# Attention blocks of two heads in turn, with the values of both heads made in one call, in a two-layer hybrid encoder trunk

## The reference, cut to what matters

```
def one_block(args):
    qi, bi = args
    qchunk = (bi * ATTN_BLOCK + jnp.arange(ATTN_BLOCK)) // CHUNK
    s = jnp.einsum('bqhd,bkhd->bhqk', qi, k, preferred_element_type=jnp.float32)
    s = jnp.where(kchunk[None, :] <= qchunk[:, None], s, -jnp.inf)
    p = jax.nn.softmax(s, axis=-1).astype(v.dtype)
    return jnp.einsum('bhqk,bkhd->bqhd', p, v)
```

## Time and profile before

| | |
|---|---|
| median of 3 runs | 1456.1 us (1455.23 to 1457.14) |
| the profiled execution's own time | 1454.87 us |
| its span in the trace | 1453.0 us |
| PE busy | 1366.1 us, 94% of the span |
| DVE, ACT, POOL busy | 774.2, 510.5, 541.4 us |
| mean granted PE clock | 0.958 of full |

### The profile page before, as it was taken

One profiled execution on the slowest core, in us unless ns is written; L12 is line 12 of the kernel. 1 busy time (PEld: TensorE's weight loads), 2 busy tenths in 40 slices (PEclk: granted clock), 3 DMA queues, 4 the chain that ended last, 5 costly groups with the idle time before them and its releaser, 6 DMA issues. The chain is left out here.

```text
span 1453.0 us, 17110 instructions
## 1 busy us (share of the span) xinstructions
PE 1366.1 (94%) x6812; PEld 1019.3 (70%) x6812; DVE 774.2 (53%) x1370; ACT 510.5 (35%) x778; POOL 541.4 (37%) x328
## 2 busy tenths in 40 slices
PE   5989899998999999899899999999899999989986
PEld 2546676776888888688655576767688888868865
DVE  5885767645667666532368646574533333321125
ACT  2523134435433333322233422253443333332322
POOL 0630100565544444344446110055744444434432
PEclk9999999898999999899999999999999999999988
DMA  9345733021665555454314451002133232322321
GB/s 384 137 116 164 155 107 117 16 87 41 212 191 180 187 192 191 139 195 153 119 60 117 78 72 45 30 30 73 44 102 101 87 102 88 101 72 88 97 63 58
DMA packets 64798, 166.76 MB, mean 115 GB/s; under 512 B 14288, under 2 KB 26960, under 8 KB 64208
## 3 DMA queue, kind: packets, MB, share of 16 engines
q1 hardware_dynamic: 64720, 165.68, 36.8%
HBM read 160.04 MB, written 5.62 MB: 114 GB/s over the span
## 5 line engine op out<-in xcount | busy, mean ns | idle before, releaser
L2044 POOL TENSOR_TENSOR ring_r<-ring,scr_r 128x1024 fp32r<-128x1024 f32 x148 | 360.2, 2435 | 441.0 <-ACT scr_r L1913 273.6
L442 PE MATMUL bank<-ym_r,scr_r 128*128 128x512 f32 x704 | 280.7, 399 | 5.3 <-DVE hm_r L1565 4.7
L444 PE MATMUL bank<-hm_r,scr_r 128*128 128x512 f32 x704 | 280.0, 398 | 0.0
L443 PE MATMUL bank<-ym_r,ring_r 128*128 128x512 f32 x704 | 277.2, 394 | 0.0
L442 PE MATMUL bank<-scr_r 128*128 128x512 f32 x480 | 197.5, 411 | 25.3 <-issue 14.2
L443 PE MATMUL bank<-scr_r,ring_r 128*128 128x512 f32 x480 | 191.0, 398 | 0.0
L1581 DVE SCALAR_TENSOR_TENSOR scr<-bank,pb,scr 128x511 f32<-128x511 f32 x88 | 66.0, 750 | 212.7 <-ACT scr L1906 212.6
L512 PE MATMUL bank<-hm,ring 128*128 128x512 f32 x352 | 168.3, 620 | 0.0
L1067 DVE SCALAR_TENSOR_TENSOR ada<-ada,silu_c 128x1024 f32<-128x1024 f32 x80 | 135.0, 1690 | 50.1 <-DMA ada<-in_w_ada 50.1
L442 PEld LDWEIGHTS bank<-ym_r,scr_r 128*128 128x128 f32 x704 | 132.7, 189 | 38.2 <-issue 6.3
L444 PEld LDWEIGHTS bank<-hm_r,scr_r 128*128 128x128 f32 x704 | 132.6, 188 | 33.2
(11 more groups left out here) (324 smaller groups left out, 1795.8 us busy)
## 6 DMA issues: line engine op xcount, KB each, us to landing
ring<-in_w_up SPq DMA_DIRECT2D x88, 512.0 KB, 3.6
ada<-in_w_ada SPq DMA_DIRECT2D x80, 512.0 KB, 3.6
ring<-in_w_down SPq DMA_DIRECT2D x44, 512.0 KB, 3.5
ring<-in_w_in SPq DMA_DIRECT2D x34, 512.0 KB, 4.5
scr<-in_w_ada SPq DMA_DIRECT2D x16, 512.0 KB, 14.3
ring<-in_w_out SPq DMA_DIRECT2D x16, 512.0 KB, 3.6
pa<-in_par_a SPq DMA_DIRECT2D x2, 2144.5 KB, 12.9
xa<-in_x SPq DMA_DIRECT2D x1, 2048.0 KB, 8.1
```

Source lines behind the costliest of these rows:

```text
L442: first = mm(dst, w_hi, x_hi, start=start, stop=False)
L443: mm(dst, w_lo, x_hi, start=False, stop=False)
L444: return first, mm(dst, w_hi, x_lo, start=False, stop=stop)
L2044: G.tensor_tensor(ring_r[:, at, :], ring[:, at, :], high[:, at, :].bitcast(F32), ALU.subtract)\
```

## The change

The blocks are taken in another order: the two heads of a pair in turn, query block by query block. `block_of(i)` gives heads 0 and 1 for i = 0 to 7, and heads 2 and 3 for i = 8 to 15, so b runs 0,0,1,1,2,2,3,3 twice where it ran 0,1,2,3 four times. The values of two blocks are made in one call `values(j)`, with the matmuls of the two heads in turn, each into its half of bank 5, and evicted by one instruction of 128 rows. A second place for a turned block is the memory of `iota`; what S5 needs of `iota` is copied out once on POOL in layer 0.

```diff
+def block_of(i):
+    return 2 * (i // 8) + i % 2, (i % 8) // 2
...
+        turned = [ptt, c_f("iota")]
...
                 def scores(i):
-                    h, b = i // NB, i % NB
+                    h, b = block_of(i)
...
-                def values(i):
-                    h, b = i // NB, i % NB
-                    pe.wait_ge(S["pt_out"], l * 16 + i + 1)
-                    if i >= 1:
-                        pe.wait_ge(S["pv_out"], l * 16 + i)
+                def values(j):
+                    h, b = block_of(2 * j)
+                    pe.wait_ge(S["pt_out"], l * 16 + 2 * j + 2)
+                    if j >= 1:
+                        pe.wait_ge(S["pv_out"], l * 8 + j)
                     for k in range(b + 1):
-                        last = mm(banks[5][64 * (h % 2):64 * (h % 2) + 64, b * P:(b + 1) * P],
-                                  vb[:, k, h * HD:(h + 1) * HD], ptt[:, k * P:(k + 1) * P],
-                                  start=(k == 0), stop=(k == b))
+                        for hp in range(2):
+                            last = mm(banks[5][64 * hp:64 * hp + 64, b * P:(b + 1) * P],
+                                      vb[:, k, (h + hp) * HD:(h + hp + 1) * HD], turned[hp][:, k * P:(k + 1) * P],
+                                      start=(k == 0), stop=(k == b))
                     last.then_inc(S["pv_mm"], 1)
...
-                    if i >= 3:
-                        values(i - 3)
+                    if i >= 4 and i % 2 == 0:
+                        values(i // 2 - 2)
...
-                    if i >= 3:
-                        h, b = (i - 3) // NB, (i - 3) % NB
-                        rows = slice(64 * (h % 2), 64 * (h % 2) + 64)
-                        a.wait_ge(S["pv_mm"], l * 16 + i - 2)
-                        A(ym[rows, 2 + h // 2, b * P:(b + 1) * P], banks[5][rows, b * P:(b + 1) * P], ACT.Identity)\
+                    if i >= 4 and i % 2 == 0:
+                        j = i // 2 - 2
+                        h, b = block_of(2 * j)
+                        a.wait_ge(S["pv_mm"], l * 8 + j + 1)
+                        A(ym[:, 2 + h // 2, b * P:(b + 1) * P], banks[5][:, b * P:(b + 1) * P], ACT.Identity)\
                             .then_inc(S["pv_out"], 1)
                     if 2 <= i < 18:
-                        b = (i - 2) % NB
+                        b = block_of(i - 2)[1]
                         a.wait_ge(S["pt_mm"], l * 16 + i - 1)
-                        A(ptt[:, 0:(b + 1) * P], banks[4][:, 0:(b + 1) * P], ACT.Identity).then_inc(S["pt_out"], 1)
+                        if i >= 4:
+                            a.wait_ge(S["pv_mm"], l * 8 + i // 2 - 1)
+                        A(turned[i % 2][:, 0:(b + 1) * P], banks[4][:, 0:(b + 1) * P], ACT.Identity).then_inc(S["pt_out"], 1)
...
-                steps = c_f("iota").rearrange("p (o c s) -> p o c s", o=1, s=SC)[:, :, :, 0]
+                steps = steps_t[:, :].rearrange("p (o c) -> p o c", o=1)
+                if l == 0:
+                    ch.link(G.tensor_copy(steps, c_f("iota").rearrange("p (o c s) -> p o c s", o=1, s=SC)[:, :, :, 0]))
```

More of the change, by code:

```diff
@@ L166, in trunk @@
         neg_half = sb("neg_half", [P, 16])
+        steps_t = sb("steps_t", [P, NSC])
         scr, scr_r = twins("scr", [P, SCRATCH])
@@ L668, in turn @@
                 def turn(i):
-                    b = i % NB
+                    b = block_of(i)[1]
                     pe.wait_ge(S["sc_norm"], l * 16 + i + 1)
@@ L798, in glu @@
                     pe.wait_ge(S["s5_gelu"], l * CT + CT)
-                    pe.wait_ge(S["pv_out"], l * 16 + 16)
+                    pe.wait_ge(S["pv_out"], l * 8 + 8)
                     wg = p_a("w_glu").rearrange("p (k n) -> p k n", n=GW)
@@ L1262, in attend @@
                 def attend(i):
-                    b, q = i % NB, i % 2
+                    b, q = block_of(i)[1], i % 2
                     if i < 16:
@@ L1271, in attend @@
                     if i:
-                        b, q = (i - 1) % NB, (i - 1) % 2
+                        b, q = block_of(i - 1)[1], (i - 1) % 2
                         v.wait_ge(S["sc_exp"], l * 16 + i)
@@ L1855, in _ @@
                 evict(AT[AU1])
-                a.wait_ge(S["pv_out"], l * 16 + 16)
+                a.wait_ge(S["pv_out"], l * 8 + 8)
                 for k in (2, 3):
```

## The result

| | before | after |
|---|---|---|
| median of the runs on one chip | 1455.76 us (8 runs) | 1445.69 us (8 runs) |
| ratio | | 0.9922 (0.9904 to 0.9941) |
| the profiled execution's own time, span | 1454.87, 1453.0 us | 1448.5, 1446.6 us |

The changed kernel is faster: the ratio is 11.4 us of 1455.76 (8.6 to 14.0). The forecast was 8.8 us less, so the direction was right and the size too small. By the ratio the time is 1444.4 us, just under the low end of the range, 1444.5. The first interval still holds 8.8 us, the second doesn't.

What follows compares the result with a forecast made beforehand. PE was taken to set the pace during attention. Layer 0 saves 0.26 + 3.48 = 3.74 us and layer 1 1.56 + 3.48 = 5.04, together 8.8, giving 1447.3 us from a median of 1456.1; range 1444.5 to 1452.0.

Steps and rivals of the forecast that it cites:

- Scores and transposes stay the same in number: PE's attention work: scores and transposes unchanged in number, transposes priced at 0.15 + 0.11 us each; only their order changes.
- 2.04 us earlier: PE up to `project(AT[I0], 0)`: fewer scores, transposes and values calls ahead of it, so it comes 2.04 us earlier.
- Values, 5.52 us a layer less: Values calls on PE: a two-head call costs what a one-head call cost, 5.52 us a layer for 11.04.
- The halves don't overlap: Rival on the values calls: only 8 x 0.14 us a layer saved, 1454.9 us in all; chance 0.04.
- each alternation pays the start of a call: Rival on the values calls: 0.36 us for each of 40 matmuls, 3.4 us a layer more, 1462.8 us; chance 0.04.
- The wait in `attend(7)`: PE's wait for ACT passes to L674; chain 0.48 us longer; ends 0.26 us earlier in layer 0, 1.56 in layer 1.
- After the wait, 3.48 us each: PE from the end of the `attend(7)` wait: the remaining 3.48 us of each layer's saving is kept there.
- The clock behind the longer wait in layer 1: Rival: PE's clock falls after the `attend(7)` wait, 1.7 to 3.4 us come back, 1449.0 to 1450.7 us; chance 0.13.
- DVE did not take over: Rival at `level(1)`, layer 0: HGRN2 levels follow DVE, layer keeps 1.2 of 3.74 us, 1449.8 us; chance 0.09.
- The full move: Rival on the `attend(7)` wait: `s_k` lands earlier by PE's gain, both layers get 5.52 us, 1445.1 us; chance 0.05.

Runs made afterwards that it cites:

- the loops changed round: Changed kernel with the two loops of `values(j)` swapped, all matmuls of one head before the other's: 1448.17 us, 0.9938 of the kernel before.
- the order alone: Kernel before with only the new order of blocks, values still one head a call: 1458.64 us, ratio 1.0019.

## Why the prediction was right or wrong

**The mechanism was right, its size too small, and two terms of the sum failed.** "Scores and transposes stay the same in number" priced the transposes as unchanged; they got 0.9 us a layer cheaper. And "2.04 us earlier" counted no clock ahead of the wait; in layer 1 the clock gave 1.6 us.

**Values, 5.52 us a layer less: right.** A call for two heads costs 0.37, 0.59, 0.81, 1.03 us, on the price taken from L834 to 0.01 us. "The halves don't overlap" and "each alternation pays the start of a call" are out; the loops changed round show the overlap once more.

**Transposes: first failed step.** The prediction priced a call at 0.15 + 0.11 each, and this 0.15 is in the chain only where a values call stands ahead. Half of the values calls are gone, so in every odd `attend(i)` with scores the transposes now stand right behind the scores, at 0.11, 0.22, 0.33 and 0.44 us for one to four. The first such row was there before the change, in `attend(2)` of layer 1, from the timeline of PE:

```profile
822.41 0.27 PE L674 MATMUL bank<-cf,scr 128*128 128x128 f32 x1
822.52 2.74 PE L512 MATMUL bank<-hm,ring 128*128 128x512 f32 x6
```

The next matmul starts 0.11 us behind the transpose. `attend(3)` and `attend(5)` save 0.15 each ahead of `project(AT[I0], 0)`, `attend(9)`, `attend(11)`, `attend(13)` and `attend(15)` behind the wait: 0.30 and 0.60 us a layer. By the sum it is thus 2.34 us up to I0 and 4.08 behind the wait, for 2.04 and 3.48. With the clock alike, the traces show 2.32 in layer 0 and 4.05 behind the wait in layer 1.

**"2.04 us earlier" up to `project(AT[I0], 0)`: second failed step.** In layer 1 it was 3.97. Of that 2.33 are work; the other 1.64 are clock, since the three matmuls behind the kernels went from 4.35 to 2.84 us and the last kernel matmuls from 0.53 to 0.40. The trace of before had them at the lower clock, in full view of the timeline, and I priced the clock only as a cost that could come on top, never as one that could go.

**The wait in `attend(7)`: right in place and releaser; its chain right, its start not.** It passed to the transposes and its releasing chain grew: from POOL's start to its end it took 48.07 - 41.88 = 6.19 us before and 46.89 - 40.16 = 6.73 after in layer 0, 45.29 - 39.11 = 6.18 and 41.91 - 35.15 = 6.76 in layer 1. That is 0.54 and 0.58 us more, for 0.48. In layer 1 the DMAs left 32.14 - 28.18 = 3.96 us earlier, just as PE was, and the wait ended 3.38 earlier (forecast 1.56): the two failed terms again, no new one. In layer 0 they left 2.58 us earlier for 0.74, and 0.89 with the slow stretch kept. There the wait ended 1.18 and 0.07 us earlier (forecast 0.26). In the first of these pairs POOL started only 1.72 us earlier, so 0.86 were lost between the first DMA and POOL; why isn't shown.

**After the wait, 3.48 us each: near in the sum, by luck.** It holds only because 1.2 us of cheaper transposes and 1.0 us of slow clock, both missing in the term, nearly cancel. The mean of two pairs is 3.99 in layer 0 and 3.21 in layer 1. In layer 1 it was 88.05 to 85.65, 2.40 us: 4.08 of work, less 1.69 of clock behind the longer wait. The clock's cost is in two rows of PE. The matmuls behind the wait took 3.01 for 1.95 us, and `hg_turn` behind them 0.63 more, before and after:

```profile
862.44 1.04 PE L545 MATMUL bank<-cf,ym 128*128 128x128 f32 x8
...
859.53 1.67 PE L551 MATMUL bank<-cf,ym 128*128 128x128 f32 x8
```

Against the second trace of before, 89.67, it was 4.02, since there the clock had fallen too (3.47 us). The clock thus cost 1.62 us there and 1.69 here, which leaves 4.09. In layer 0 it was 3.68, and 4.30 between the second traces. Those 0.6 us are the clock as well: `hg_turn` took 1.32 and 1.90 us in the first traces, 1.21 and 1.14 in the second.

**The rivals.** The clock behind the longer wait in layer 1 did fall in both traces of after, near the price that the rival gave it (1.67 us). But before has that too in one of two, so it is no difference that can be put down to the change. The Trainium skill, TensorE: Matmul & The Clock Gate, The HAM clock gate, says that the number of slow matmuls at a kernel's start varies from run to run. These traces show the like in the middle of a kernel, with 1.95 and 3.47 us behind 1.66 and 1.76 us of idleness in one program. DVE did not take over, with 0.14 us to spare. The full move did not happen: the chain's 0.5 us was paid.

**The account.** Means of two traces each: layer 0 is 4.6 us shorter (forecast 3.74) and layer 1 6.6 (forecast 5.04). Of the 2.4 us between 11.2 and 8.8, 1.8 come from the end of the wait in layer 1 (3.40 for 1.56), 0.4 from that in layer 0, and 0.2 from behind the waits. By cause: in layer 1 ahead of the wait the clock gave 1.6 us and the transposes 0.3; behind the two waits the transposes gave 1.2, and the clock took 1.0 of it back. It stays open what makes the clock fall behind the kernels: it came in every trace of before and of the order alone, went in layer 1 of every trace of after whose kernels started at 16.97 or 16.98 (five of five; in layer 0 in one of three), came back with 1.71 us of padding, and neither an earlier place nor dense work among the kernels removed it.

## What to carry to other kernels

Two matmuls of 64 output channels into the two halves of the array cost here what one costs, 0.22 us; issue them in turn, and evict both at once. When calls fall away, look also at what the call behind each of them paid for standing there (here 0.15 us): a row without the neighbour gives the price. Read a trace of before for stretches at the lower clock ahead of the edit, not only behind it: a step that moves them by a us or two can take such a stretch away or bring one, and a sum of durations doesn't hold it, so put it into the range on both sides. Where an engine waits for a DMA, look at what stands ahead of it in its queue: eight DMAs moved up past one load gained 9.3 us in the kernel before, nearly as much as the whole change, and with it 21.6 us (1.5%).

## What the runs showed of the hardware

Two groups of matmuls into different halves overlap where they meet even when issued one after the other: 4 and 4 took 1.52 us, 1.03 in turn, 1.9 by the sum. Fewer than three a head lost nothing.

Transposes of 128 columns cost 0.11 us each right behind scores and 0.15 us more in all behind a values call (0.11 and 0.26 for one). What makes the 0.15 isn't shown.

With PE busy without a break, the granted clock fell from 2.4 to 1.2 GHz near the end of 32 matmuls of 16 columns, and the three matmuls of 512 columns behind them took 4.35 to 4.54 us for 2.84. The three matmuls had this in both layers of both traces of before; in the kernel after, layer 0 had it in one trace of two.
